# Cross attention in a fused two-layer kernel: keys and queries as stacked pieces, scores and values as three rounded products

## The reference

```python
def cross_attention(xn, mem_n, w_q, w_kv, w_o):
    q = (xn @ w_q).reshape(b, s, X_HEADS, X_HEAD_DIM)
    kv = mem_n @ w_kv
    logits = jnp.einsum('bshd,bmhd->bhsm', q, k).astype(jnp.float32) * X_HEAD_DIM ** -0.5
    p = jax.nn.softmax(logits, axis=-1)
    o = jnp.einsum('bhsm,bmhd->bshd', p.astype(v.dtype), v).reshape(b, s, X_HEADS * X_HEAD_DIM)
    return o @ w_o
x = x + cross_attention(rms_norm(x, xattn_norm_g[l]), rms_norm(mem, mem_norm_g[l]), ...)
```

## Time and profile before

| | us |
|---|---|
| median of 3 runs | 1034.8 (1034.38 to 1035.12) |
| profiled execution, first to last instruction | 1032.7 |
| TensorE matmul busy | 1025.3 |
| VectorE busy | 745.9 |
| ScalarE busy | 600.2 |

### The profile page before, as it was taken

The page is one execution under the profiler, slowest core; times in us unless marked ns, Lnnn a source line. Parts: engine busy times, 40 slices in busy tenths (PEclk is TensorE's granted clock), DMA queues, the critical chain, the costliest instruction groups (busy, mean ns, idle before and its releaser), DMA issues.

```text
span 1032.7 us, 17606 instructions
## 1 busy us (share of the span) xinstructions
PE 1025.3 (99%) x7580; PEld 930.5 (90%) x7580; DVE 745.9 (72%) x891; ACT 600.2 (58%) x720; POOL 4.7 (0%) x9
## 2 busy tenths in 40 slices
PE   9999999999999999999999999999999999999998
PEld 8999877899988988888889989999999888888887
DVE  5677765676653688776568999689948988776456
ACT  6575466436344465554557996699755665555443
POOL 1000000000000000000000000000000000000000
PEclk9999999999999999999999999999999999999999
DMA  9985544744535476655565556356454566654741
GB/s 298 267 233 171 163 154 129 247 165 161 206 122 163 156 231 195 190 186 176 186 201 164 164 164 193 94 164 185 144 164 153 163 206 203 203 186 145 229 154 41
DMA packets 141469, 183.83 MB, mean 178 GB/s; under 512 B 14148, under 2 KB 92080, under 8 KB 141136
## 3 DMA queue, kind: packets, MB, share of 16 engines
q1 hardware_dynamic: 141032, 181.45, 55.4%
q10 hardware_dynamic: 360, 1.25, 0.3%
HBM read 180.40 MB, written 2.29 MB: 177 GB/s over the span
## 4 chain that ended last, share of the span: by engine, by line
PE 94%; DVE 4%; ACT 1%; issue 1%; DVEq 0%; ACTq 0%
PE ps L552 28%; PE ps L585 22%; PE ps L634 16%; PE ps L587 11%; PE ps L678 2%; PE ps L1174 2%; PE ps L582 1%; PE ps L680 1%; DVE wlo L1870 1%; PE ps L819 1%; PE ps L1039 1%; PE ps L602 1%; PE ps L918 1%; PE ps L940 1%; PE ps L790 1%
## 5 line engine op out<-in xcount | busy, mean ns | idle before, releaser
L1870 DVE TENSOR_TENSOR wlo<-raw,whi 128x2048 fp32r<-128x2048 f32 (+3 forms) x170 | 378.2, 2228 | 144.5 <-ACT whi L1234 143.8
L1234 ACT ACTIVATE whi<-raw 128x2048 fp32r<-128x2048 f32 (+1 forms) x167 | 310.5, 1864 | 86.5 <-PE ps L552 32.0
L552 PE MATMUL ps<-ha,whi 128*128 128x256 f32 x1264 | 231.5, 285 | 0.5 <-DVE gb L2468 0.5
L585 PE MATMUL ps<-ha,whi 128*128 128x512 f32 x640 | 222.7, 393 | 0.0
L552 PEld LDWEIGHTS ps<-ha,whi 128*128 128x128 f32 x1264 | 197.2, 192 | 2.6 <-DVE wlo L1870 0.8
L552 PE MATMUL ps<-ha,wlo 128*128 128x256 f32 x632 | 178.8, 283 | 0.0
L587 PE MATMUL ps<-ha,wlo 128*128 128x256 f32 x640 | 178.3, 279 | 0.0
L585 PEld LDWEIGHTS ps<-ha,whi 128*128 128x128 f32 x640 | 119.9, 187 | 27.1
L552 PEld LDWEIGHTS ps<-ha,wlo 128*128 128x128 f32 x632 | 121.1, 192 | 0.0
L587 PEld LDWEIGHTS ps<-ha,wlo 128*128 128x128 f32 x640 | 120.5, 188 | 0.1
L585 PE MATMUL ps<-pr,whi 128*128 128x512 f32 x330 | 115.3, 393 | 0.0
(11 more groups left out here) (400 smaller groups left out, 1683.6 us busy)
## 6 DMA issues: line engine op xcount, KB each, us to landing
raw<-in_w_in SPq DMA_DIRECT2D x54, 1024.0 KB, 5.3
raw<-in_w_ffn_gate SPq DMA_DIRECT2D x11, 1024.0 KB, 5.2
raw<-in_w_ffn_up SPq DMA_DIRECT2D x11, 1024.0 KB, 5.1
raw<-in_w_gate SPq DMA_DIRECT2D x11, 1024.0 KB, 5.1
raw<-in_w_up SPq DMA_DIRECT2D x11, 1024.0 KB, 5.2
raw<-in_w_xkv SPq DMA_DIRECT2D x8, 1024.0 KB, 5.0
raw<-in_w_ffn_down SPq DMA_DIRECT2D x8, 1024.0 KB, 5.0
raw<-in_w_down SPq DMA_DIRECT2D x8, 1024.0 KB, 5.2
```

Of the source, the lines that this page charges most:

```text
L552: mm = e.matmul(ps[0:width, m * T:(m + 1) * T], a[:, kk, m * width:(m + 1) * width], b[:, off + k, :], start=k == 0 and j == 0 and m % 2 = ...
L585: e.matmul(banks[s][:, at_:at_ + 512], wh[:, kk, c], H[2][:, :, k, :], start=k == 0, stop=False, skip_group_check=True)
L1234: e.activation(h, r, ACT.Copy).then_inc(*hi_done.up(n))
L1870: e.tensor_tensor(l, r, h.bitcast(F32), ALU.subtract).then_inc(*lo_done.up(n))
```

## The change

- Keys and queries are made as eight pieces of 256 columns, `mk0` to `mk3` and `xq0` to `xq3`, one unit of weights each. The keys' banks alternate between 2 and 3, the queries' between 1 and 0, so the third key piece waits for VectorE's first add of `mk0`.
- A new step `joined` for each piece: ScalarE copies one of the two sums to `join`, VectorE adds the other, ScalarE copies the sum to a rounded high part, VectorE subtracts for the low part.
- Scores and values are three rounded products of 256 columns in place of one in float32; probabilities and values get a low part on VectorE (`xpt_lo`, `xv_lo`). The probabilities of head 1 are turned into another half bank than those of the others.
- The memory rows are scaled by ScalarE before they are turned. `diagonal`, `rows_of` and the copy to `Rm` of the memory go. The first turn stands behind the first half of the value projection `fv`.
- The queries' row scale is not applied to them: it is held per token (`xr`) and used as the scale of the exponential and of the maximum. The sums of squares for it are two matmuls of one column.

```diff
-    MN = (at("mn_hi", [P, 8, T], F32R, 144), at("mn_lo", [P, 8, T], F32R, 152))
-    xK = at("xk", [P, 8, T], F32, 120)
-    xV = at("xv", [P, 2, 1024], F32, 128)
+    MN = pair("mn", 8, 144)
+    xK = (at("xk_hi", [P, 8, T], F32R, 120), at("xk_lo", [P, 8, T], F32R, 172))
+    xV = (at("xv_hi", [P, 2, 1024], F32R, 128), at("xv_lo", [P, 2, 1024], F32R, 136))
+    join = [at(f"join{i}", [P, 2, T], F32, 200 + 2 * i) for i in range(2)]
...
-    U["mk0"], U["mk1"] = (cols(w_kv, 512 * i, 512, 8) for i in range(2))
-    U["xq0"], U["xq1"] = (cols(flat("w_xq"), 512 * i, 512, 8) for i in range(2))
+    for i in range(4):
+        U[f"mk{i}"] = cols(w_kv, 256 * i, 256, 8)
+    for i in range(4):
+        U[f"xq{i}"] = cols(flat("w_xq"), 256 * i, 256, 8)
+    CROSS = [f"mk{i}" for i in range(4)] + [f"xq{i}" for i in range(4)]
+    CROSS_BANK = dict(zip(CROSS, (2, 3, 2, 3, 1, 0, 1, 0)))
...
-        e.wait_ge(s_m[0], 16)
-        e.wait_ge(*v_stat.on(("rows", "x")))
-        turn("mem", m_tm, 3, 0, v_stat.on("gains b"))
         e.wait_ge(*a_evac.on(("x", 1)))
         unit_tm("fv", 0, HA, 2, v_split.on(("x", 3)))
+        e.wait_ge(*v_stat.on(("rows", "x")))
+        e.wait_ge(*a_stat.on("memory scaled"))
+        turn("mem", m_tm, 3, 0, v_stat.on("gains b"))
         unit_tm("fv", 1, HA, 2)
...
-        rows_of("mem", 3, v_split.on(("mem", 3)))
+        e.wait_ge(*v_split.on(("mem", 3)))
...
-            if h % 2 == 0:
-                e.wait_ge(*v_evac.on(f"xq{h // 2}"))
+            e.wait_ge(*v_split.on(f"mk{h}"))
+            e.wait_ge(*v_split.on(f"xq{h}"))
...
-                    mm = e.matmul(S[:, t_ * T:(t_ + 1) * T], xq[:, 2 * h + j, t_ * P:(t_ + 1) * P], xK[:, 2 * h + j, :],
-                                  start=j == 0 and t_ == 0, stop=j == 1, skip_group_check=True)
+                    for n, (a, b) in enumerate(((0, 0), (0, 1), (1, 0))):
+                        mm = e.matmul(S[:, t_ * T:(t_ + 1) * T], xq[a][:, 2 * h + j, t_ * P:(t_ + 1) * P],
+                                      xK[b][:, 2 * h + j, :], start=j == 0 and t_ == 0 and n == 0,
+                                      stop=j == 1 and n == 2, skip_group_check=True)
...
-        linear("mk0", MN, 2, None, v_evac.on("br12"))
-        linear("mk1", MN, 3, None, v_split.on(("mg", 1)))
-        unit("xq0", 0, HA, 1, h_ready("mo"), v_evac.on(("mo", 3)))
-        column_sums("xattn", nsq, 2, v_evac.on("mk0"), v_stat.on(("fold", "xattn")))
-        unit("xq0", 1, HA, 1, h_ready("mo"))
-        linear("xq1", HA, 0, None, v_evac.on(("mo", 1)))
+        cross_free = dict(zip(CROSS, (v_evac.on("br12"), v_split.on(("mg", 1)), v_evac.on("mk0"), v_evac.on("mk1"),
+                                      v_evac.on(("mo", 3)), v_evac.on(("mo", 1)), v_evac.on("xq0"), v_evac.on("xq1"))))
+        for name in CROSS:
+            piece(name, MN if name in CROSS[:4] else HA, CROSS_BANK[name], h_ready("mo") if name == "xq0" else None,
+                  cross_free[name])
+            if name == "xq0":
+                e.wait_ge(*v_evac.on("mk2"))
+                e.wait_ge(*v_stat.on(("fold", "xattn")))
+                for t_ in range(2):
+                    mm = e.matmul(banks[2][:, t_:t_ + 1], nsq[:, 0, t_ * P:(t_ + 1) * P], ones[:, 0:1], start=t_ == 0,
+                                  stop=True, skip_group_check=True)
+                mm.then_inc(*pe_sum.up(("sums", "xattn")))
...
+        rs_tm("mem", m_tm, 20)
+        e.wait_ge(*a_stat.on(("rs", "mem")))
+        for t_ in range(2):
+            mm = e.activation(m_tm[:, t_, :], m_tm[:, t_, :], ACT.Copy, scale=sc[:, 20 + t_:21 + t_])
+        mm.then_inc(*a_stat.up("memory scaled"))
+        hi_for("fv")
         norm_hi("mem", MN, "mem_norm_g", 3, 0)
-        hi_for("fv")
...
+        def joined(p):
+            name, t = CROSS[p], join[p % 2]
+            dst = (xK if p < 4 else xq)[0][:, 2 * (p % 4):2 * (p % 4) + 2, :]
+            e.wait_ge(*whole(name))
+            if p >= 2:
+                e.wait_ge(*v_split.on(CROSS[p - 2]))
+            e.activation(t[:, :, :], split_sums(CROSS_BANK[name])[1], ACT.Copy).then_inc(*a_evac.up(name))
+            e.wait_ge(*v_evac.on(name))
+            e.activation(dst, t[:, :, :], ACT.Copy).then_inc(*a_split.up(name))
...
+                                  scale=xr_scale[:, t_:t_ + 1], accum_out=mx[:, 2 + t_:3 + t_])
...
-        lo_for("mk0")
-        fold("xattn", nsq)
-        evac("mk0", 2, xK[:, 0:4, :], Rm)
-        lo_for("mk1")
-        evac("mk1", 3, xK[:, 4:8, :], Rm)
...
+            e.tensor_tensor(t[:, :, :], split_sums(CROSS_BANK[name])[0], t[:, :, :], ALU.add).then_inc(*v_evac.up(name))
...
+            split_lo(name, hi_x[:, k_, :], lo_x[:, k_, :], t[:, :, :])
+
+        for p in range(1, 8):
+            lo(U[CROSS[p]][0][0] + 2)
+            if p == 1:
+                fold("xattn", nsq)
+            joined(p - 1)
...
+        def xv_lo(i):
+            c = slice(512 * i, 512 * i + 512)
+            e.wait_ge(*a_evac.on((f"mv{i}", 1)))
+            for t_ in range(2):
+                mm = e.tensor_tensor(xV[1][:, t_, c], tokens(1 - i)[:, t_, :], xV[0][:, t_, c].bitcast(F32), ALU.subtract)
+            mm.then_inc(*v_split.up(f"mv{i}"))
```

More of the change, by code:

```diff
@@ L476, in sync @@
             fetch_for_pair(e, fetch, "mo", k)
-        fetch_for("mk0", "mk1", "xq0", "xq1", "mv0", "mv1")
+        fetch_for(*CROSS, "mv0", "mv1")
         for k in range(2):
@@ L939, in x_values @@
                 for kt in range(2):
-                    mm = e.matmul(O[:, dt_ * T:(dt_ + 1) * T], xV[:, kt, h * 256 + dt_ * P:h * 256 + (dt_ + 1) * P],
-                                  xPT[h % 2][:, kt, :], start=kt == 0 and dt_ == 0, stop=kt == 1, skip_group_check=True)
+                    for n, (a, b) in enumerate(((0, 0), (0, 1), (1, 0))):
+                        mm = e.matmul(O[:, dt_ * T:(dt_ + 1) * T], xV[a][:, kt, h * 256 + dt_ * P:h * 256 + (dt_ + 1) * P],
+                                      xPT[h % 2][b][:, kt, :], start=kt == 0 and dt_ == 0 and n == 0,
+                                      stop=kt == 1 and n == 2, skip_group_check=True)
             mm.then_inc(*pe_val.up(("cross", h)))
@@ L962, in tensor @@
         unit_tm("mv0", 1, MN, 1)
-        unit_tm("mv1", 0, MN, 0, v_evac.on("xq1"))
+        unit_tm("mv1", 0, MN, 0, v_evac.on("xq3"))
         x_values(0)
@@ L1331, in scalar @@
         e.dma_start(x_kept, X[:, :, :]).then_inc(s_kept, 16)
+        e.wait_ge(*pe_sum.on("rows x"))
+        for i in range(2):
+            e.wait_ge(s_m[i], 16)
+        rs_tm("mem", m_tm, 20)
[4 more added lines that the diff above has]
+        hi_for("fv")
         norm_hi("mem", MN, "mem_norm_g", 3, 0)
-        hi_for("fv")
         e.wait_ge(*whole("fv"))
@@ L1342, in scalar @@
         hi(U["svf"][0][0] + 2)
-        e.wait_ge(*pe_sum.on("rows x"))
-        rs_tm("mem", m_tm, 20)
         hi(U["svf"][1][0] + 2)
@@ L1454, in scalar @@
         hi(U["mk0"][0][0])
-        hi(U["mk0"][1][0])
+        hi(U["mk1"][0][0])
         add_into("mo", lambda c: g_col("xattn_norm_g", c))
@@ L1459, in scalar @@
         squares("xattn", X, nsq, lambda g: v_evac.on(("mo", g)))
-        hi(U["mk0"][1][0] + 2)
-        hi_for("mk1")
-        hi(U["xq0"][0][0] + 2)
-        inverse_root("xattn", Rw[:, :], banks[2][:, 0:T], pe_sum.on(("sums", "xattn")))
+        def joined(p):
[8 more added lines that the diff above has]
+        for p in range(1, 8):
+            hi(U[CROSS[p]][0][0] + 2)
+            joined(p - 1)
+            if p == 5:
+                inverse_root("xattn", xr, banks[2][:, 0:2], pe_sum.on(("sums", "xattn")))
+        joined(7)
         def x_softmax(h):
@@ L1482, in ox_hi @@
             e.activation(OX[0][:, 2 * h:2 * h + 2, :], wide(x_out(h)), ACT.Copy).then_inc(*a_split.up(("ox", h)))
-        hi(U["xq0"][1][0] + 2)
-        hi_for("xq1")
         x_softmax(0)
@@ L2143, in vector @@
         lo(U["mk0"][0][0])
-        lo(U["mk0"][1][0])
+        lo(U["mk1"][0][0])
         e.wait_ge(s_x2, 16)
@@ L2147, in vector, with joined @@
         add_half("mo", "mo1", 1, 1, lambda c: g_col("xattn_norm_g", c))
-        e.wait_ge(*v_stat.on(("rows", "mem")))
-        lo_for("mk0")
-        fold("xattn", nsq)
-        evac("mk0", 2, xK[:, 0:4, :], Rm)
-        lo_for("mk1")
-        evac("mk1", 3, xK[:, 4:8, :], Rm)
-        lo(U["xq0"][0][0] + 2)
-        lo(U["xq0"][1][0] + 2)
-        e.wait_ge(*a_stat.on(("r", "xattn")))
-        evac("xq0", 1, xq[:, 0:4, :], Rw, 0.0625)
+        lo(U["mk0"][0][0] + 2)
+        def joined(p):
+            name, t = CROSS[p], join[p % 2]
+            k_ = slice(2 * (p % 4), 2 * (p % 4) + 2)
+            hi_x, lo_x = xK if p < 4 else xq
+            e.wait_ge(*a_evac.on(name))
+            e.tensor_tensor(t[:, :, :], split_sums(CROSS_BANK[name])[0], t[:, :, :], ALU.add).then_inc(*v_evac.up(name))
+            e.wait_ge(*v_evac.on(name))
+            if p == 4:
+                e.wait_ge(*pe_sum.on(("sums", "xattn")))
```

(14 more changed lines are left out.)

56 lines of the change are left out of this document (31 added, 25 removed).

## The result

The changed kernel took 1040.7 us (median of 5 runs, 1037.9 to 1041.8) beside 1034.4 us for the kernel before (5 runs, 1034.0 to 1035.1): ratio 1.005, 95% interval 1.0038 to 1.0061. By the ratio it is slower by about 5 us, by the medians by 6.3; 1036.2 us and no change were forecast, and 1040.7 lies outside the range of 1034.8 to 1038.6. The profiled execution took 1040.73 us, with a span of 1038.9.

What follows compares the result with a forecast made beforehand. TensorE was taken to bound the kernel, matmuls open for 1025.3 of 1032.7 us. Terms -1.8 - 2.3 - 0.45 + 5.7 + 0.3 = +1.4 on 1034.8 gave 1036.2 us, no change; range 1034.8 to 1038.6 for 8 in 10.

Steps and rivals of the forecast that it cites:

- pieces, with the norm's sums: Key and query projections: matmuls of 512 and 256 columns replace three of 256, -1.8 us; norm's sums no gain.
- products: Scores and values: three rounded products at 0.360 us replace float32 at 0.432, 32 times, -2.3 us.
- memory: Memory scaled by ScalarE ahead of its turn: the row matmuls of its scale leave TensorE's chain, -0.45 us.
- wait for the join: Third key piece waits for bank 2 until VectorE's first joining add; TensorE stands from 254.8 to 260.5, +5.7 us.
- other joins: The other seven joins of the projections: rate holds but twice 0.1 us or none to spare, +0.3 us, bounds 0 and 0.6.
- clock: Rival: clock falls in the gap before the third key piece, 1.6 us more, 1037.8 us; chance 0.37.
- The formula of the Trainium skill: Projection matmuls: N/2.4 + 2.5 ns each, so pieces gain 0.3 us; set aside for the trace's rows.

Runs made afterwards that it cites:

- busy_gap: The changed kernel with 23 thrown-away matmuls of 128 columns filling TensorE's gap ahead of the third key piece: 1038.4 us, ratio 1.0019.
- fp32_products: The changed kernel with each group of three rounded products put back to one float32 product of the first halves: 1041.5 us, ratio 1.006.
- gap_before: The kernel before with one wait more: the second half of the keys held until VectorE has evicted the first: 1044.2 us, ratio 1.0076.
- after_again: The changed kernel once more, with nothing altered: 1039.9 us, ratio 1.0043 to the kernel before.
- join_first: The changed kernel with each join ahead of the next weight copy and split, and the fold behind the third add: 1033.2 us, ratio 0.9986.
- waits_out: join_first with the values' halves ahead of the next weight split, and the lower bounds' exponential behind the key weights' split: 1031.3 us, ratio 0.9963.
- fold_late: The changed kernel with only the three folds of the squares moved behind the first joining add: 1036.2 us, ratio 1.0001.
- no_waits: fold_late's order by mistake for join_first's, with values' splits ahead of the next weight split and the start's exponential later: 1036.5 us, ratio 1.0012.
- ws_one: The kernel before with one of the eight turns of the mixer's weights in the first layer's feed-forward: 1037.0 us, ratio 1.0015.
- other_banks: The changed kernel, order kept, with four banks in rotation instead of two for the key and query pieces: 1034.5 us, ratio 0.9996.

## Why the prediction was wrong

Term by term, in the trace of the changed kernel:

| step | forecast us | measured us | from |
|---|---|---|---|
| pieces, with the norm's sums | -1.8 | -1.2 | busy_gap, see below |
| products | -2.3 | -2.4 | chain; fp32_products |
| memory | -0.45 | -0.2 | first key piece 243.5 against 243.70 |
| wait for the join | +5.7 | +5.4 | TensorE's waits |
| other joins | +0.3 | 0 | TensorE's waits |
| clock | 0 (rival: +1.6) | +2.1 | busy_gap |
| sum | +1.4 | +3.7 | stage's end 337.28 against 333.58 |

- **The step that failed is the one that left the clock out.** The gap was foreseen with its place, releaser and length. Its consequence was put among the rivals, with "against it that the clock reads full in every slice here" and 240 us of dense work ahead. Those say nothing on a gap that was not there yet. The only evidence in the trace on an array that had stood was the start, and it spoke for the fall. gap_before shows that the fall comes with the gap, busy_gap that it goes when the gap is filled. The rival had the mechanism and 1037.8 us, beside 1038.0 in the lower group. Its price of 1.6 us was 0.5 short: it counted 16 records of 128 columns at 0.099 us each, where some 12 records of 512 and 256 columns ran at the low clock, a pair in 0.64 us instead of 0.35.
- **Pieces: the size was off, because the row was from another stretch.** The pace of 0.346 was read in the feed-forward. The first 32 pairs here ran at 0.353 (11.3 us for two pieces, where two units took 11.5). In busy_gap the other 96 ran at 0.347, and six pieces and the sums took 34.0 us against 35.0 (6 x 5.76 + 0.43). That gives 0.2 + 1.0 = 1.2. In the changed kernel itself only the last 48 and in after_again the last 89 had this pace; in the first profile some 40 behind the low clock ran at 0.353, so of its 2.1 us for the clock some 0.3 are pace. In join_first, which has no gap, all 128 ran at 0.353: from the first piece to the scores' first record it took 45.7 us (244.10 to 289.78) against 46.5 (243.70 to 290.20), 0.8 in all. The formula of the Trainium skill that the prediction quotes (TensorE: Matmul & The Clock Gate, "Back-to-back issue gap") gave 0.3 as an estimate; the rows give 0.9 at the one pace and 1.7 at the other, so no run here bears it out.
- **Products: right.** 2.4 us off the chain, none hidden.
- **Memory: the term was right, its cover too thin.** The row matmuls are gone and TensorE did not wait at the memory's turn; where nothing else waits, the keys start 0.4 us sooner (waits_out). But with the turn moved behind the first value unit, that unit is wanted 0.87 us sooner. The prediction gave its low weights 0.6 us to spare (33.1 against 33.7) from one execution. In two of the profiles (this one and join_first) that spare was eaten: ScalarE's copy waited 1.1 and 1.3 us for its transfer, where it waited 0.7 or less in all others, and TensorE then waited 0.5 and 0.6 us. This profile's start was besides 0.4 us early in TensorE's first turns (5.57 where the earlier trace rows have 6.00), so the -0.2 is read against a shifted start.
- **Other joins: within their bounds.** None was late. In busy_gap, where the clock holds, the adds of mk1, xq0 and xq1 end 0.3, 0.9 and 0.4 us ahead of the pieces that need their banks; forecast were 0.1, 0.8 and 0. The values' low half ended 0.7 us ahead of the values in the changed kernel, as forecast (0.8), but only because of the gap: in join_first, which has none, it was late by 1.5.
- **What no step held: the pace of the executions.** 3.7 us on 1034.4 is 1038.1, inside the range, and two of the five runs took 1037.9 and 1038.0. The other three lie about 3 us higher; the profiled one is of these, and it has the slow pace behind 400 us. The five runs of the kernel before beside them all lie in its lower group, but of its later ones 19 of 29, 9 of 23, 8 of 29 and 5 of 12 lie in the upper. The measured ratio of 1.005 thus holds the change's own +3.7 us and the difference in groups. Whether that is an uneven draw or the change makes the slow pace likelier is not shown: only 2 of the 10 runs of the changed kernel lie near 1038.0, where 57 of 98 of the kernel before lie in its lower group. The forecast's bound of 0.2% for what can be told from no change was too small: the two groups of this kernel alone lie about 2.6 us apart.

Cause and cure of the 3.7 us are shown by runs. For the pace behind 400 us the profiles show where the two part, at the first piece that follows the one behind the turns; what makes it come out one way or the other stays open.

## What to carry to other kernels

When a stage is cut into pieces that share fewer accumulator banks, the operation that frees a bank takes on a due time that it did not have: put it ahead of splits and folds that are wanted later, or alternate over more banks. Price a new stall of TensorE at its length plus the slow work behind it, here 5.4 + 2.1 us, and remove it first, or fill it. Read a pace in the stretch where the work will run, and look at single executions for groups before a change of a few tenths of a per cent is put down to an edit.

## What the runs showed of the hardware

- The granted clock fell to 0.50 at gaps of 5.4, 5.7 and 3.0 us. The gap of 3.0 stands in two runs: in fold_late the clock was still 1.00 when work resumed, in no_waits it had fallen. Filled with small matmuls, the same gap of 5.4 us left it at 1.00. The price behind a gap was 2.1 us in the changed kernel and 1.6 in fold_late.
- A pair of one 512-column and one 256-column matmul paces at 0.346 or at 0.353 us, at a granted clock of 1.00, with durations of 391 to 394 or 398 ns for the longer one. It holds for over 100 us. In these profiles it changes where the stream is broken or a piece begins. In the 14 profiles the 16 pairs behind the turns are always slow, and those from the next piece on are of either pace. By the groups of times they were slow in all 12 runs of ws_one, fast in all 11 of other_banks and mixed in the kernel before. One profile from each of its groups puts the distance between them, 2.5 us, down to this.
- Seven turns less made the kernel before 2.7 us slower than its own lower group, by the slow pace and a wait of 0.5 us.
